# Where a mixer's parameter chain, a dense stage's tables and an attention's query halves stand in the order of work

## The reference

```python
z = rmsnorm(h, mix_norm_g)
p = z @ w_in                                   # u | q, f, v, og | a, b (gates)
y_a = s5_mixer(p[..., :o1], ...)
y_b = hgrn2_mixer(p[..., o1:o2], ...)          # 8 heads of 128, chunks of 16
merged = sigmoid(p[..., o5:o6]) * (y_a @ w_ssm_proj) + sigmoid(p[..., o6:]) * (y_b @ w_hgrn_proj)
h = h + merged @ w_out
...                                            # a feed-forward part follows
def s5_mixer(u, ...):
    dt = exp(log_dt)
    mag = exp(lr * dt)
    ab_re, ab_im = mag * cos(li * dt), mag * sin(li * dt)
    coef_re = ((ab_re - 1) * lr + ab_im * li) / (lr * lr + li * li)      # coef_im likewise
    bb_re = coef_re * b_re - coef_im * b_im                              # bb_im likewise
    ...                                        # a linear recurrence with ab over the tokens, then c, d, gelu, w_glu
```

## Time and profile before

| what | value |
| --- | --- |
| median of 3 runs | 3454.78 us (3453.41 to 3455.07) |
| the profiled execution | 3446.28 us, its span 3444.5 us |
| TensorE busy | 3168.6 us, 92% of the span, 20182 instructions |
| VectorE busy | 1987.2 us, 58% |
| ScalarE busy | 923.7 us, 27% |
| GpSimd busy | 224.8 us, 7% |
| mean granted clock of TensorE | 0.952 of full speed |

### The profile page before, as it was taken

One profiled execution on the slowest core, in us unless ns is written; L12 is line 12 of the kernel. 1 busy time (PEld: TensorE's weight loads), 2 busy tenths in 40 slices (PEclk: granted clock), 3 DMA queues, 4 the chain that ended last, 5 costly groups with the idle time before them and its releaser, 6 DMA issues. The chain is left out here.

```text
span 3444.5 us, 47716 instructions
## 1 busy us (share of the span) xinstructions
PE 3168.6 (92%) x20182; PEld 2925.0 (85%) x20182; DVE 1987.2 (58%) x2796; ACT 923.7 (27%) x1301; POOL 224.8 (7%) x226
## 2 busy tenths in 40 slices
PE   7999999998786999999999999999898977998787
PEld 7999999997765999999999999899898964555465
DVE  6665666665885655574465377444545526666446
ACT  5222222222331411211111111221323224444323
POOL 0000000000044000000000000000031001222200
PEclk9999999998878999999999999999999988999998
DMA  4223323233452443212212313211121330000132
GB/s 137 89 91 105 95 83 98 84 93 132 122 56 40 164 133 133 74 51 97 98 50 80 104 47 126 72 41 45 55 70 55 137 127 0 1 1 1 50 114 71
DMA packets 100669, 277.35 MB, mean 81 GB/s; under 512 B 13412, under 2 KB 32356, under 8 KB 100200
## 3 DMA queue, kind: packets, MB, share of 16 engines
q1 hardware_dynamic: 100456, 274.30, 24.9%
HBM read 214.60 MB, written 59.65 MB: 80 GB/s over the span
## 5 line engine op out<-in xcount | busy, mean ns | idle before, releaser
L427 PE MATMUL mixer_in_dense<-mix_z_high,mixer_in_whigh 128*128 128x348 f32 x1312 | 431.4, 329 | 15.2 <-DVE mixer_in_wlow L521 10.3
L427 PE MATMUL mixer_in_dense<-mix_z_high,mixer_in_wlow 128*128 128x348 f32 x1312 | 427.2, 326 | 0.0
L427 PE MATMUL mixer_in_dense<-mix_z_low,mixer_in_whigh 128*128 128x348 f32 x1312 | 426.2, 325 | 0.0
L1412 PE MATMUL flow_dense<-rst_norms_operand_b_high,flow_whigh 128*128 128x342 f32 x1248 | 399.2, 320 | 0.4 <-DVE flow_wlow L1505 0.4
L1412 PE MATMUL flow_dense<-irst_norms_operand_b_low,flow_whigh 128*128 128x342 f32 x1248 | 398.3, 319 | 0.0
L1412 PE MATMUL flow_dense<-rst_norms_operand_b_high,flow_wlow 128*128 128x342 f32 x1248 | 397.5, 318 | 0.0
L1975 PE MATMUL joint_dense<-rst_norms_operand_b_high,joint_whigh 128*128 128x342 f32 (+2 forms) x1056 | 344.6, 326 | 18.5 <-DVEq L2092 10.1
L1975 PE MATMUL joint_dense<-rst_norms_operand_b_high,joint_wlow 128*128 128x342 f32 (+2 forms) x1056 | 341.4, 323 | 0.0
L1975 PE MATMUL joint_dense<-irst_norms_operand_b_low,joint_whigh 128*128 128x342 f32 (+2 forms) x1056 | 340.5, 322 | 0.0
L1412 PE MATMUL flow_dense<-first_operand_a_high,flow_whigh 128*128 128x342 f32 (+1 forms) x912 | 291.8, 320 | 16.8 <-DVEq L1526 16.8
L1412 PE MATMUL flow_dense<-first_operand_a_low,flow_whigh 128*128 128x342 f32 (+1 forms) x912 | 292.2, 320 | 0.0
(11 more groups left out here) (572 smaller groups left out, 5969.4 us busy)
## 6 DMA issues: line engine op xcount, KB each, us to landing
mixer_in_wstage<-w_in SPq DMA_DIRECT2D x56, 512.0 KB, 4.6
mixer_in_mod_w<-w_mod SPq DMA_DIRECT2D x64, 384.0 KB, 3.6
first_norms_weights<-w_up SPq DMA_DIRECT2D x44, 512.0 KB, 3.4
flow_side<-h SPq DMA_DIRECT2D x24, 512.0 KB, 5.0
h<-flow_out SPq DMA_DIRECT2D x24, 512.0 KB, 3.5
first_norms_weights<-ab_w_in SPq DMA_DIRECT2D x20, 512.0 KB, 3.5
p<-mixer_in_out SPq DMA_DIRECT2D x16, 528.0 KB, 2.9
first_norms_weights<-w_down SPq DMA_DIRECT2D x16, 512.0 KB, 3.5
```

The source lines that it names most:

```text
L427: mm = pe.matmul(bank(s)[:, 0:W], a[n % 2][:, P * m:P * (m + 1)], z[x][:, m, W * b:W * (b + 1)], start=m == 0 and i == 0, stop=m == DT - 1 ...
L1412: mm = pe.matmul(o, w[n % NW][:, P * k:P * (k + 1)], x[h][:, k, where], start=k == 0 and e == 0, stop=k == kt - 1 and e == 2)
```

## The change

It has three parts.

First, the small parameter pieces leave heads_out. `mix_schedule` puts them, as ("param", name, k), at the free slots f+6, 10, 12, 16, 18 and 20 of heads 1 to 4, one piece to a slot. VectorE, ScalarE and SyncE get them in `mix_heads`: the loads of log_dt, lam_re and lam_im come on SyncE behind the first two modulation weights. Their results live in a new outer phase "s5" that holds both the mixer and a phase "ssm" with heads_out and the scan; the latter was the phase "s5" before. So one more phase ends behind the scan.

Second, heads_out has new tables of slots, one for VectorE and one for ScalarE, and VectorE takes the low half before the pieces of its slot.

Third, `made_at` in the attention: the query halves of the next head are made in steps 0 and 1 (before: both in step 0), the three key pieces all in step 2 (before: two in step 1, one in step 2).

```diff
@@ mix_schedule
+    chain = [("step", 0), ("angles", 0), ("base", 0)] + [("power", k) for k in range(2, TAU + 1)]
+    chain += [("reverse", 0), ("turns", 0), ("rotation", 0), ("rotation", 1), ("rotation", 2), ("negate", 0),
+              ("coefficients", 0), ("coefficients", 1)]
+    free = [last["f", h] + d for h in range(1, 5) for d in (6, 10, 12, 16, 18, 20)]
+    for s, (name, k) in zip(free, chain):
+        at.setdefault(s, []).append(("param", name, k))
@@ mix_heads, SyncE
                 mod_load(0)
                 mod_load(1)
+                for buf, n in ((dt, "log_dt"), (lr, "lam_re"), (li, "lam_im")):
+                    sp.dma_start(buf[:, :], t[n]).then_inc(steps_in, 16)
@@ mix_heads, ScalarE (VectorE's param() has the operations that heads_out had, L883 to L959)
+                def param(name):
+                    if name == "step":
+                        act.wait_ge(steps_in, 48)
+                        act.activation(dt[:, :], dt[:, :], ACT.Exp).then_inc(dt_ready, 1)
+                    elif name == "base":
+                        act.wait_ge(angled, 1)
+                        act.activation(mag[:, :], x1[:, :], ACT.Exp).then_inc(mag_ready, 1)
+                        act.wait_ge(reduced, 1)
+                        act.activation(si[:, :], r[:, :], ACT.Sin).then_inc(sines, 1)
+                        act.activation(co[:, :], ab[:, :], ACT.Sin).then_inc(sines, 1)
+                    elif name == "reverse":
+                        act.wait_ge(powered, 1)
+                        for q_ in range(2):
+                            for j in range(TAU):
+                                act.activation(pwt[:, q_, :, j], pw[:, q_, TAU - 1 - j, :], ACT.Copy)
@@ heads_out
-    at = {}
-    for s, name, k in ((-8, "step", 0), (-7, "angles", 0), (-5, "base", 0), (-4, "power", 2), (-3, "power", 3),
-                       (-2, "power", 4), (-1, "power", 5), (-1, "power", 6), (-1, "power", 7), (-1, "power", 8),
-                       (1, "turns", 0), (2, "rotation", 0), (2, "reverse", 0), (3, "coefficients", 0), (4, "table", 0),
-                       (5, "negate", 0), (5, "scaled_b", 0), (6, "vectors", 0), (7, "table", 1), (8, "outer", 1),
-                       (9, "outer", 2), (11, "outer", 3), (12, "outer", 4), (14, "outer", 5), (15, "outer", 6),
-                       (17, "outer", 7), (19, "outer", 8), (20, "outer", 0), (21, "skip", 0)):
+    at, at_act = {}, {}
+    for s, name, k in ((3, "vectors", 0), (5, "table", 0), (7, "outer", 1), (8, "outer", 2), (10, "outer", 3),
+                       (11, "outer", 4), (13, "outer", 5), (14, "outer", 6), (16, "outer", 7), (17, "outer", 8),
+                       (18, "scaled_b", 0), (20, "table", 1), (21, "skip", 0)):
         at.setdefault(s, []).append((name, k))
+    for s, name, k in ((7, "table", 0), (10, "outer", 0), (22, "table", 1)):
+        at_act.setdefault(s, []).append((name, k))
@@ heads_out, SyncE
                 load(0)
-                for buf, n in steps_of:
-                    sp.dma_start(buf[:], t[n]).then_inc(steps_in, 16)
@@ heads_out, VectorE
                 for s in range(NS):
+                    n, b = divmod(s, 3)
                     if s == 1:
                         low(2)
+                    if n >= 2 and b == 1 and n + 1 < DT:
+                        low(n + 1)
                     for name, k in at.get(s, ()):
                         piece(name, k)
-                    n, b = divmod(s, 3)
-                    if n >= 2 and b == 1 and n + 1 < DT:
-                        low(n + 1)
@@ attend, made_at
-        return ((("q", h + 1, 0), ("q", h + 1, 1)), (("k", h + 1, 0), ("k", h + 1, 1)), (("k", h + 1, 2),), ())[j]
+        return ((("q", h + 1, 0),), (("q", h + 1, 1),), (("k", h + 1, 0), ("k", h + 1, 1), ("k", h + 1, 2)), ())[j]
```

More of the change, by code:

```diff
@@ L238, in mix_heads @@
         squares, root = w("mean_squares", 9), w("inverse_root", 9)
+        lr, li, dt, th, kk, r, ab, co, si, mag, x1, x2 = (ph.sb(n, (P, NP)) for n in (
+            "lr", "li", "dt", "th", "kk", "r", "ab", "co", "si", "mag", "x1", "x2"))
+        pw, pwt, rot, m8, turn, x3, x4 = (params[n] for n in (
+            "powers", "powers_reversed", "rot", "m8", "turn", "coef_re", "coef_im"))
         pd = [ph.ps(f"dense{j}", (P, 512)) for j in range(2)]
@@ L386, in _ @@
                     for piece, h, _k in at.get(s, ()):
-                        if piece == "sigmoid":
+                        if piece == "param":
+                            param(h)
+                        elif piece == "sigmoid":
                             act.wait_ge(moved, last["f", h] + 1)
@@ L550, in _ @@
                     for piece, h, k_ in at.get(s, ()):
-                        if piece == "decay":
+                        if piece == "param":
+                            param(h, k_)
+                        elif piece == "decay":
                             if h == 0:
@@ L784, in piece @@
                 def piece(name, k):
-                    if name == "step":
-                        act.wait_ge(steps_in, 16 * len(steps_of))
-                        act.activation(dt[:, :], dt[:, :], ACT.Exp).then_inc(dt_ready, 1)
-                    elif name == "angles":
-                        act.wait_ge(angled, 1)
-                        act.activation(mag[:, :], x1[:, :], ACT.Exp).then_inc(grown, 1)
-                    elif name == "base":
-                        act.wait_ge(reduced, 1)
-                        act.activation(si[:, :], r[:, :], ACT.Sin).then_inc(sines, 1)
-                        act.activation(co[:, :], ab[:, :], ACT.Sin).then_inc(sines, 1)
[L795 to L799, removed]
-                        ins.then_inc(reversed_, 1)
-                    elif name == "table":
+                    if name == "table":
                         act.wait_ge(wrapped, k + 1)
@@ L820, in _ @@
                     act.activation(x[0][:, m, FIRST:FIRST + NM], ring[m % 4][:, :], ACT.Copy).then_inc(x_high, 1)
-                    for name, k in at.get(m - HH, ()):
+                for s in range(NS):
+                    n, b = divmod(s, 3)
+                    for name, k in at_act.get(s, ()):
                         piece(name, k)
-                for s in range(NS):
-                    for name, k in at.get(s, ()):
-                        piece(name, k)
-                    n, b = divmod(s, 3)
                     if b == 0:
```

185 lines of the change are left out of this document (92 added, 93 removed).

## The result

The changed kernel takes 3427.43 us (median of 5 runs, 3415.81 to 3433.81) against 3454.78 (3453.41 to 3455.30): 27 us less, ratio 0.992 with a 95% interval of 0.9899 to 0.9941. Run again beside other kernels it gave 3425.44 (6 runs, 3418.70 to 3434.54) against 3452.52, ratio 0.9927 (0.9914 to 0.994). The forecast was 3427. Two things in this are not as forecast, though: the scatter, 18 us where the kernel before had 2 (and 9 over 21 later runs), and where the time went. The profiled execution took 3415.81 us, 30.5 less than that of before.

The account below looks back on a forecast made before the run. TensorE, busy 92% of the span, was taken as the bound, so gains had to be its idle time or slow clock. -14.7 -1.4 +0 +0.5 -12.2 = -27.8 us from the median 3454.8 gave 3427, range 3413 to 3441.

Parts of the forecast that it names:

- heads_out, main stretch: After the opening's end, T, a 14.17 us idle stretch goes and a 1.35 us wait comes: -14.7 us, bounds -15.7 to -13.
- heads_out, start: Three parameter loads no longer stand between the first weights and first heads' rows: -1.4 us, bounds 0 and -2.4.
- Mixer: Some 90 small VectorE instructions move into the mixer, mostly in VectorE's idle time: 0 us, at most 3 in all.
- One more phase: One more barrier of all engines between scan and first: +0.5 us, bounds 0 and 1.5.
- Attention: Query halves and keys of the next head made in other steps: -12.2 us over heads 1 to 6, bounds 0 to -20.
- Step 2: Attention step with three keys, the third waiting 0.9 us for the first one's buffer: 12.9 us, now 9.64, so +3.25.
- Steps 1: Attention steps with one query half instead of two before VectorE's maximum: 10.8 us odd, 13.6 even; -3.7 and -2.8.
- rival (b): Attention gives about twice: step 2 at 11.5 us, no slow clock in step 1; 3414 us. Chance 0.13.
- (d): Slower: in the attention's keys' step the ring hands out one buffer at a time, +35 us; 3462 us. Chance 0.04.
- (c): heads_out's wait is divided over five tiles, by late weights or VectorE's work per tile: 8 us back, 3435. Chance 0.05.
- (a): The attention gives nothing, the keys' step eating what the other steps give: 3439 us. Chance 0.15.
- (e): The change does not reach heads_out's wait, something other than the order holding low 3: 3450 or so. Chance 0.02.

Follow-up runs that it names:

- second trace: The changed kernel profiled again with no edit; heads_out took 106.9 us against 103.5 in its first trace; 3425.44 us, ratio 0.9927.
- run 2: The changed kernel with the attention's old order of query halves and keys; 3444.08 us, ratio 0.9969 against the kernel before.

## Why the prediction was right, and where it was not

**heads_out, main stretch: right.** -14.9 measured (85.4 to 70.5), -14.7 forecast, with the new wait in its place. What the forecast took as one number is a scatter: the landing of one load decides between 1.03 and 2.66. In the second trace the last product ends at T+73.8, 11.6 us sooner than before, and so outside the bound of -13 (1.35+1.7): the bound had the slow stretch, but not a wait of 2.66 with it.

**heads_out, start: -1.0 for -1.4.** Timelines of SyncE's queue and ScalarE after, against the earlier trace rows:

```profile
811.69 0.34 SPq L831 DMA_DIRECT2D heads_out_wstage<-w_hgrn_proj  x1
812.08 0.42 SPq L837 DMA_DIRECT2D heads_out_a<-yb  x1
...
816.98 1.06 ACT L895 ACTIVATE heads_out_yb_high<-heads_out_a 128x1026 fp32r<-128x1026 f32 x1 [0.25 <-DMA heads_out_a<-yb]
```

From the first issue of the phase to ScalarE's first rows it is 5.29 us, before 6.27 (818.20 to 824.47). The three loads are gone (the rows are issued 0.39 behind the weights), but the first rows now reach ScalarE 4.9 us after their issue instead of 4.45. That is one pair of traces: in the ten with the moved loads it is 4.8 to 5.3 us, in the four without 6.3 to 7.0, means 5.1 and 6.6, so the forecast of -1.4 fits them better than it fits this pair.

**Mixer: the 0 was right for the chain, but for 0.3 us.** Heads without a slow stretch last 96.1 us in both kernels, with 60 us of VectorE before and 62 to 66 after where the chain has pieces. The one place singled out did show: TensorE's products behind the second S chain wait, 0.09 us (190.20 to 190.29) for the 0 to 0.1 forecast. That head takes 96.4 us at full clock in six traces with the chain and 96.1 in all four without it; what makes the other 0.2 us is not shown.

```profile
189.88 0.32 PE L460 MATMUL mixer_in_dense<-mix_z_low,mixer_in_whigh 128*128 128x348 f32 x1
190.29 0.35 PE L516 MATMUL mixer_in_scores_and_out<-mixer_in_vt,mixer_in_st 128*128 128x128 f32 x1
```

**One more phase: +0.3 to +0.5 for +0.5.**

**Attention: the failed term, -7.7 for -12.2.** The step that failed reads "Step 2: starts with the second half's 3.8 us still on VectorE, x = 4.2", where x is how late VectorE's maximum starts after the step's scores. x is 5.3 (3097.50 to 3102.83): VectorE starts 2.0 us after the half's first product, as forecast, but needs 4.7 for the half. Timelines of VectorE and GpSimd in step 2 of head 5, and of TensorE at that step's end:

```profile
3098.11 0.69 DVE L2710 TENSOR_TENSOR attn_turned_sin<-attn_turned,attn_turn 32x512 f32<-32x512 f32 x1 [0.25 <-PE attn_turned L2518]
3098.83 0.69 DVE L2711 TENSOR_TENSOR attn_turned_cos<-attn_turned,attn_turn 32x512 f32<-32x512 f32 x1
3099.55 1.58 DVE L2712 TENSOR_TENSOR attn_turned_cos<-attn_turned_cos,attn_turned_sin 32x512 f32<-32x512 f32 x1
...
3102.83 2.89 DVE L2752 TENSOR_REDUCE attn_max<-attn_scores 128x1 f32<-128x1280 f32 x2
...
3097.95 2.65 POOL L2794 TENSOR_SCALAR attn_probs<-attn_probs,attn_inverse_sum 128x1280 f32<-128x1280 f32 x2 [9.13 <-DVE attn_inverse_sum L2768]
...
3110.54 0.65 PE L2523 MATMUL attn_turned<-attn_ckv,attn_wk 128*64 128x256 f32 x2 [0.59 <-DVEq L2728]
```

One operation (L2712, L2704 before) takes 1.58 instead of 0.68, while GpSimd normalises probabilities beside it. Over heads 1 to 6 by lines, after and before, the mean is 1140 ns for 683, since it is every second one; these 5.5 us are VectorE's longer busy time:

```profile
L2712 DVE TENSOR_TENSOR attn_turned_cos<-attn_turned_cos,attn_turned_sin 32x512 f32<-32x512 f32 x12 | 13.7, 1140 | 0.4
```

```profile
L2704 DVE TENSOR_TENSOR attn_turned_cos<-attn_turned_cos,attn_turned_sin 32x512 f32<-32x512 f32 x12 | 8.2, 683 | 0.4
```

The ring's wait, 0.59, was smaller than the 0.9 forecast. Together step 2 is 13.6 for 12.9. By step, all of heads 1 to 6, from the first scores product of a step to that of the next:

| step | forecast | first trace |
| --- | --- | --- |
| 0 | -9.4 | -12.2 |
| 1 | -19.5 | -19.0 |
| 2 | +19.5 | +23.9 |
| 3 | -3.0 | -3.4 |
| sum | -12.4 (written -12.2) | -10.6 |

Steps 2 cost 4.4 us more than forecast, and steps 0 gave 2.8 back, most of it in heads 3 and 5, where they had a slow stretch before (13.86 us at a clock of 0.88) and none after (11.2). Steps 1 came out as forecast, because the lengths of 10.8 and 13.6 were worked out from VectorE's work and so hold no slow stretch; rival (b) counted that stretch a second time. The rest is head 0, taken as "about 0": its steps 1 to 3 grew from 29.6 to 32.7 us, mainly step 2, from 7.5 to 12.6. This step has no value sums yet, so it was shorter than the other heads' before, and all three keys and a ring's wait of 0.95 us now stand in it.

**The sum** was within 3 us of the profiled execution (3418.5 for 3415.8) because two errors cancelled: 4.5 us too much from the attention, and 6.6 us that the mixer's clock gave in this execution (its stage's 7.6 less the start's 1.0), which the forecast had at 0. For the median no such table exists, and the median itself is not known to 1 us: the second set of runs is 25 us below the kernel before by its ratio, the first 27. The mechanisms were right but for step 2 and head 0; the agreement to 1 us was luck. Of the rivals, (d) is excluded by the 0.59, (c) came true in small, (a), (b) and (e) are not what happened.

## What to carry to other kernels

Where an engine is the bound for a stretch, a wait it suffers early comes out at the stretch's end, at another line: read its busy share over the whole stretch, and move a large piece past the last deadline rather than trimming the order within a slot. When work moves in time, look at what the engines beside it do at its new time (here GpSimd), and not only at what waits for it. A sum can come out right by two wrong terms, so check it by stage.

## What the runs showed of the hardware

**The clock falls or not at the same place of the same work.** Two heads of the mixer before and two after, by windows (columns as in the earlier trace rows):

```profile
304.54:403.78 99.24, 98.32 (x718) 96.16 (x719) 59.77 (x94) 24.95 (x42) 0.00 (x0) 0.97 0.29 91
503.06:599.19 96.13, 95.16 (x718) 93.00 (x718) 59.80 (x94) 25.44 (x43) 0.00 (x0) 1.00 0.30 94
```

```profile
304.31:400.42 96.11, 95.16 (x719) 93.01 (x719) 65.90 (x132) 27.02 (x59) 0.00 (x0) 1.00 0.31 94
594.22:693.49 99.27, 98.29 (x718) 96.14 (x719) 59.79 (x94) 25.08 (x42) 0.00 (x0) 0.97 0.29 92
```

The same code costs 96.1 or 99.3 us, and between them lies the clock alone. In all 14 traces the six full heads have one of three lengths, 96.1, 97.7 or 99.3 us at a clock of 1.00, 0.98 or 0.97 (0.3 more in the head named above). Closer, the end of one and the same head, before and after: the stretch in which TensorE turns v and makes 18 products of two columns each for the modulation, and the stretch behind it.

```profile
312.70:316.10 3.40, 2.92 (x24) 2.67 (x23) 2.86 (x4) 0.00 (x0) 0.00 (x0) 1.00 0.38 50
316.10:322.90 6.80, 6.80 (x27) 6.80 (x27) 0.00 (x0) 0.00 (x0) 0.00 (x0) 0.50 0.55 192
```

```profile
312.50:315.90 3.40, 2.90 (x25) 2.64 (x23) 2.82 (x4) 0.00 (x0) 0.00 (x0) 1.00 0.37 52
315.90:322.70 6.80, 6.80 (x46) 6.80 (x47) 0.69 (x2) 1.97 (x2) 0.00 (x0) 1.00 0.63 230
```

The first rows of both kernels are alike (2.92 and 2.90 us busy, 24 and 25 products, clock 1.00). Behind them the kernel before runs at 0.50 for 6.8 us, 27 products instead of 46; the changed one doesn't. Nor does the chain in this head decide: in run 2, with the very same mixer code, the head took 99.25 us. What decides is not shown. So the mixer took 808.8 to 820.5 us in ten traces with the moved chain (mean 813.0) and 814.4 to 819.3 in four without it (mean 817.0), and whether the chain moves the odds stays open. TensorE was 99% busy in these heads, and its longest idle gap in them, over both traces, is 0.53 us. The Trainium skill (TensorE: Matmul & The Clock Gate, section "Why this matters for your kernels") connects a fall with idle gaps, longer than any here; the trace does not agree.

**VectorE held up by GpSimd.** An addition of two SBUF tiles (L2712 above) stands 16 times in each of the 14 traces. It took 1.57 to 1.61 us instead of 0.68 in the 45 instances where a GpSimd operation had started 0.3 us before it, and ended 0.53 to 0.54 us behind that operation each time; in the other 179, where GpSimd was idle, about to end, or began just behind it, it took 0.68, but for two of 0.71 and 0.74. The multiplications before it, which read PSUM and SBUF, kept their 0.69 or 0.70 beside the same GpSimd work. No run took GpSimd's operation away, so this rests on instances that came together. The Trainium skill says that of VectorE with two SBUF inputs and a GpSimd operation that reads SBUF, the one that comes second is blocked until the first ends (SBUF — State Buffer, section "SBUF: two separate sides"). The trace agrees: GpSimd ends at 3100.60, the addition 0.5 us later.
